# Expert rows on one core: own selection steps spread over more rows, the next selection from a later row, queries six rows apart

## What is computed

```python
def peer(h, w_query, sub_keys, u_tab, v_tab):
    def block_fn(xb):                                    # xb: tokens x 1024
        qry = (xb @ w_query).reshape(P, PEER_HEADS, 2, PEER_HALF)
        s = jnp.einsum('phcd,hckd->phck', qry, sub_keys)
        top_s, top_i = lax.top_k(s, PEER_TOPK)
        cand_s = top_s[..., 0, :, None] + top_s[..., 1, None, :]
        cand_i = top_i[..., 0, :, None] * PEER_N_KEYS + top_i[..., 1, None, :]
        best_s, pos = lax.top_k(cand_s.reshape(P, PEER_HEADS, -1), PEER_TOPK)
        idx = jnp.take_along_axis(cand_i.reshape(P, PEER_HEADS, -1), pos, axis=-1)
        gate = jax.nn.softmax(best_s, axis=-1)
        act = jax.nn.gelu(jnp.einsum('pd,phkd->phk', xb, u_tab[idx]))
        return jnp.einsum('phk,phkd->pd', gate * act, v_tab[idx])
```

## Time and profile before

| | us |
|---|---|
| median of three runs | 4306.75 (4305.49 to 4308.24) |
| the profiled execution, its own time | 4312.35 |
| its span, first to last instruction | 4310.6 |
| PE, DVE, ACT, POOL busy | 3531.4, 2658.5, 1401.6, 1209.2 |
| DMA traffic over the span | 1088.29 MB, 252 GB/s mean |
| layer 0's rows, first to last dot | 2044.8 to 3418.5 |
| layer 1's rows, first to last dot | 3623.5 to 4296.8 |

### The profile page before, as it was taken

How to read it: one execution, slowest core, us unless ns; L and a number is a source line. 1 busy time by engine, 2 the same in 40 slices (tenths; PEclk the granted TensorE clock), 3 DMA queues, 4 the chain that set the end, 5 groups by cost and what they waited for, 6 DMA issues and landing times.

```text
span 4310.6 us, 38816 instructions
## 1 busy us (share of the span) xinstructions
PE 3531.4 (82%) x11382; PEld 1864.0 (43%) x11382; DVE 2658.5 (62%) x5456; ACT 1401.6 (33%) x3747; POOL 1209.2 (28%) x1228
## 2 busy tenths in 40 slices
PE   7888978999867677778989887777888787777877
PEld 3334436844335555567545432322233255322222
DVE  3656455849656666634967577667555455786444
ACT  1231120004424544431333333433433221333333
POOL 0001100001005444520333333343435201434432
PEclk9888989999979998999999999999999998999999
DMA  5523324635321111043999999999999724999998
GB/s 214 194 78 134 120 88 171 227 149 194 130 70 33 52 52 57 23 169 150 363 379 373 371 421 421 407 418 421 410 418 416 328 79 147 387 421 421 409 421 362
DMA packets 169765, 1088.29 MB, mean 252 GB/s; under 512 B 16432, under 2 KB 45488, under 8 KB 51152
## 3 DMA queue, kind: packets, MB, share of 16 engines
q0 software_dynamic: 112608, 820.04, 46.5%
q1 hardware_dynamic: 56944, 265.77, 16.8%
HBM read 1075.19 MB, written 10.55 MB: 252 GB/s over the span
## 4 chain that ended last, share of the span: by engine, by line
PE 37%; DMA 20%; DVE 20%; issue 11%; POOL 6%; ACT 6%; DVEq 0%; SPq 0%; POOLq 0%; ACTq 0%
PE bank L199 20%; DMA arena<-in_uv,arena 17%; PE bank L2977 6%; ACT arena L211 5%; POOL arena L3009 5%; DVE arena L3026 4%; DVE arena L443 2%; PE bank L1620 2%; DVE arena L561 2%; PE bank L2454 2%; DVE arena L217 1%; PE bank L2151 1%; PE bank L2143 1%; DMA arena<-in_w_rows 1%; DMA arena<-in_wq 1%
## 5 line engine op out<-in xcount | busy, mean ns | idle before, releaser
L2977 PE MATMUL bank<-arena 128*128 128x512 f32 x3072 | 1499.6, 622 | 356.8 <-ACT arena L211 355.5
L211 ACT ACTIVATE arena<-arena 128x1 f32<-128x1 f32 (+4 forms) x2831 | 949.6, 335 | 2024.9 <-DVE arena L3026 1136.9
L199 PE MATMUL bank<-arena 128*128 128x256 f32 (+4 forms) x4640 | 1304.1, 440 | 79.8 <-ACT arena L211 33.4
L3026 DVE CUSTOM_DVE_ANT_0 arena<-arena 128x1024 f32<-128x1024 f32 x768 | 941.2, 1226 | 631.1 <-DMA arena<-in_uv,arena 602.3
L3009 POOL DMA_INDIRECT arena<-in_uv,arena x768 | 791.9, 1031 | 1289.7 <-PE bank L2977 880.5
L2977 PEld LDWEIGHTS bank<-arena 128*128 128x128 f32 x3072 | 547.9, 193 | 1281.0 <-ACT arena L211 829.3
L199 PEld LDWEIGHTS bank<-arena 128*128 128x128 f32 (+2 forms) x4640 | 808.3, 196 | 564.9 <-issue 427.4
L211 ACT ACTIVATE arena<-bank 128x512 f32<-128x512 f32 (+4 forms) x306 | 160.8, 525 | 508.9 <-PE bank L199 324.4
L443 DVE CUSTOM_DVE_ANT_0 arena<-arena 128x1024 f32<-128x1024 f32 x192 | 241.0, 1255 | 33.3 <-DMA arena<-in_w_rows 21.6
L211 ACT ACTIVATE arena<-bank,arena 128x128 f32<-128x128 f32 (+1 forms) x400 | 162.4, 406 | 290.5 <-PE bank L2143 228.1
L626 POOL TENSOR_SCALAR arena<-arena 128x1 f32<-128x1 f32 (+3 forms) x48 | 16.9, 353 | 655.6 <-ACT arena L211 459.8
(11 more groups left out here) (251 smaller groups left out, 2505.5 us busy)
## 6 DMA issues: line engine op xcount, KB each, us to landing
arena<-in_w_rows SPq DMA_DIRECT2D x50, 1024.0 KB, 5.1
arena<-in_w_in SPq DMA_DIRECT2D x16, 2048.0 KB, 7.9
arena<-in_wq SPq DMA_DIRECT2D x14, 2048.0 KB, 8.5
arena<-in_dn_w SPq DMA_DIRECT2D x12, 2048.0 KB, 10.1
arena<-in_w_up SPq DMA_DIRECT2D x11, 2048.0 KB, 8.1
arena<-in_dn_wo SPq DMA_DIRECT2D x8, 2048.0 KB, 11.0
arena<-in_w_rows POOLq DMA_DIRECT2D x14, 1024.0 KB, 5.5
arena<-decay_rest SPq DMA_DIRECT2D x56, 256.0 KB, 5.1
```

Of the source, the lines that this page charges most:

```text
L199: t = p.e.matmul(out, l, r, start=(i == 0), stop=(i == n - 1))
L211: return a().activation(out, in_, f, **kw)
L2977: t = p.e.matmul(by[half], m["dg"][ee % 4], m["uv"][r][:, 1024 + 512 * half:1536 + 512 * half], start=(ee == 0), stop=(ee == 127))
L3026: v().tensor_tensor_reduce(self.spare, uv[:, 0:1024], m["ht"][n % 2], 1.0, 0.0, ALU.mult, ALU.add, m["acts"][:, ee:ee + 1]).then_inc(*V.up ...
```

## The change

Four tables of numbers move instructions, nothing is computed otherwise.

- Own steps of tile 0 (both layers): two in every third row and one in the others (4 in 3 rows), so layer 0's end in row 54 instead of 36 and layer 1's in row 33 instead of 22.
- Tile 1's selection starts at row 60 of tile 0 instead of 40 (layer 0), with 5 steps in 3 rows instead of 5 in 4; in layer 1 at row 36 instead of 28, with 5 in 4 as before.
- Of the late steps the queries stand six rows apart from row 78 on (78 to 174) instead of four from row 76 (76 to 140). The projection and the norm stay.
- So tile 2's selection starts at row 48 of tile 1 instead of 14, with 3 steps in 2 rows instead of one a row. Every selection still hands out its indices about where it did (rows 119 and 114 against 119 and 113).

```diff
-    LATE = dict([(10 + 6 * j, j) for j in range(8)] + [(10 + 8 * 6 + 2 * j, 8 + j) for j in range(9)]
-                + [(10 + 8 * 6 + 18 + 4 * j, 17 + j) for j in range(17)])
+    LATE = dict([(10 + 6 * j, j) for j in range(8)] + [(58 + 2 * j, 8 + j) for j in range(9)]
+                + [(78 + 6 * j, 17 + j) for j in range(17)])
...
     def own_gate_row(self, layer, group):
 
-        return (self.gate_step(0, group) - self.FIRST_STEPS[layer] + 1) // 2 - 1
+        wanted = self.gate_step(0, group) - self.FIRST_STEPS[layer]
+        row = 0
+        while row + (row + 2) // 3 < wanted:
+            row += 1
+        return row - 1
+
+    def own_steps(self, ee):
+
+        return 2 if ee % 3 == 0 else 1
 
     def select_row(self, layer, n):
 
-        return {(0, 0): 40, (0, 1): max(8, max(self.LATE) - 126), (1, 0): 28}.get((layer, n), 8)
+        return {(0, 0): 60, (0, 1): max(8, max(self.LATE) - 126), (1, 0): 36}.get((layer, n), 8)
 
     def ahead_steps(self, layer, n, ee):
 
         if ee < self.select_row(layer, n):
             return 0
-        return 2 if n == 0 and ee % 4 == 0 else 1
+        once = {(0, 0): ee % 3 == 0, (0, 1): ee % 2 == 1, (1, 0): ee % 4 > 0}.get((layer, n), True)
+        return 1 if once else 2
...
                 if n == 0:
-                    for _ in range(2):
+                    for _ in range(self.own_steps(ee)):
                         next(first, None)
```

## The result

| | before | after |
|---|---|---|
| median | 4306.12 us (4304.95 to 4308.24, 4 runs) | 4277.98 us (4277.05 to 4283.94, 4 runs) |
| ratio | | 0.9931, 95% interval 0.9918 to 0.9943 |
| the profiled execution, its own time | 4312.35 | 4277.18 |
| its span | 4310.6 | 4275.4 |
| layer 0's rows, first to last dot | 1373.7 (2044.8 to 3418.5) | 1348.5 (2041.3 to 3389.8) |

The change gained 28.1 us between the medians. In the two profiled executions the rows themselves are 25.2 us shorter in layer 0 and 4.1 in layer 1, 29.3 together. The spans differ by 35.2; the 5.9 beyond the rows lie ahead of them and between the layers, where both programs are the same, so they aren't the change's.

A forecast was written before the change was run, and what follows sets the result against it. The DMA bounds the kernel, so only its idle stretches in the row stages, 37 us by busy share, can be gained. 2.2 + 5.9 + 2.8 + 2.5 - 0.5 + 4.5 = 17.4 us takes 4306.75 to 4289.4, range 4280 to 4302.

The forecast's parts named there:

- Parts 3, 4 and 5: Rows 60 to 119: denser DVE, weight wait gone, 8.3 us idle becomes 5.5 (gain 2.8); tile boundary: gain 2.5.
- Part 3's density: Layer 0, rows 60 to 119: selection in 60 rows; DVE needs 166 us, DMA 154 to 159, DVE 7 to 12 over.
- the slack: Gather buffers: DVE, ACT and PE together may be delayed 7.3 us free; only what is over it idles the DMA.
- Part 1: Tile 0's own steps, 4 in 3 rows: idle of 9.4 us becomes 7.2, gain 2.2 (0 to 4), capped by PE.
- Part 2: Tile 1's selection from row 60 instead of 40: idle of 7.4 us becomes 1.5, gain 5.9 (2.9 to 7.4).
- Part 5's cost in tile 1: Tile 1, 1.5 selection steps a row: 2.45 us a row on average, inside the slack, cost 0.5 us (0 to 2).
- Part 6: Layer 1, own steps 4 in 3 rows and select at row 36: idle 5.5 us becomes 1, gain 4.5 (1.5 to 5.5).
- DVE as the bound: Rival, rows 60 to 119: step costs or waits above the mean, idle 13 to 17 us, 4297 to 4301; chance 0.2.
- PE as the bound: Rival, rows 10 to 58: PE blocks at every late projection, gain 12, 4295; chance inside the forecast's 0.65.
- a wait for the weights that stays: Rival: load slower behind fuller gather queues (over 15 us), 2.8 and 2.5 go, 4295; chance inside the forecast's 0.65.
- Slower through query blocks: Rival, query rows up to 120: each 3.6 us query block costs its full length, 34 us idle, 4318; chance 0.05.
- All slack is used well: Rival: idle in rows 60 to 119 falls to 1 us and the select costs nothing, 4282; better case's chance 0.05.

The follow-up runs named there:

- The probes: Changed kernel with extra work of known length on DVE or on PE in layer 1's second tile; that tile takes 330.6 and 329.0 us against 315.1.
- experiment 1: Kernel before with only the queries six rows apart, and tile 2's selection from row 48 of tile 1; 4294.65 us against 4308.77, ratio 0.9967.
- experiment 7: Changed kernel with its queries four rows apart again from row 78; 4298.37 us, ratio 0.9970 to the kernel before.
- experiment 8: Changed kernel with its queries five rows apart from row 78; 4282.57 us, ratio 0.9939 to the kernel before.
- 9 and 12: Changed kernel, no query from row 121 to tile 1's row 2, then five apart, tile 2's selection at row 50; 4271.85 and 4271.34 us.
- experiment 2: Kernel before with only tile 1's selection moved to row 60, 5 steps in 3 rows; 4304.63 us, ratio 0.9991.

## Why the prediction was wrong

The sign, the places and most of the mechanisms held; the size didn't. The median lies only 2 us under the range, and 4279.95 when measured again, at its edge; but the gain was 28.1 us where 17.4 was forecast. In the rows, 29.3 less 17.4 is 11.9: the share's own reading is 22.6, so 5.2 us of this are terms that were too small in the prediction's own unit, and 6.7 are what the unit leaves out.

**The first failed step is the measure**, "So I count only what the DMA stands idle in the row stages, as width x (1 - share / 1.01)". The rows have the rate in their last column. By it the same five stretches have lost 12.2, 9.3, 14.3, 9.3 and 8.6 us, 54 instead of 37. The probes show that the share misses part of the time. The Trainium skill, "Perfetto Trace Analysis", Identifying the Most-Contended Engine, says that for DMA one should take the utilization of HBM instead of occupancy, since with 16 engines the latter misleads. The trace agrees: of 29.3 us between the dots the share shows 22.6.

**The second is what was put in place of the waits for the weights**: an idle of 5.5 us for DVE's excess in 2280 to 2400, and 4 at the boundary. By the share the changed kernel loses 2.7 in rows 80 to 120 and 2.3 in rows 0 to 20 of tile 1. And by the rate there was more to gain: the stretch with two of the three waits had lost 14.3 where the prediction has 8.3, and 2430 to 2460, behind the third, 9.3 where it has 6.5. Parts 3, 4 and 5 with tile 1's cost gave 2.8 + 2.5 - 0.5 = 4.8 us; the queries alone gave 14.2 (experiment 1), and taken out of the change they cost 16.8 (experiment 7). This is the largest term that was mis-sized, and it alone is about as large as the miss of 10.7 us between the medians.

**Part 3's density** was sized right as a sum and wrong as a price. Rows 60 to 119 took 164.9 us (2212.6 to 2377.5) where DVE's sum was 166, with 148.67 of DVE busy. But in these rows the changed kernel loses 1.4 + 5.1 + 0.9 = 7.4 us by the rate and 2.8 by the share, and experiment 1, with the old, sparser selection, loses 3.3 + 1.9 in rows 80 to 120 and next to nothing in 60 to 80: the density costs some 2 us, not the 7 to 12 less the slack. Nor did it stretch POOL's gather issues there, the second price. POOL's gathers alone in rows 60 to 119, before and after:

```profile
2230.40:2403.90 173.50, 69.68 (x58) 0.95 0.96 384
...
2212.60:2377.50 164.90, 63.29 (x60) 1.00 0.99 402
```

That is 1.20 us for an issue before and 1.05 after. What stretches an issue the traces do tell: before, the 42 issues whose first 0.93 us lay almost wholly (0.90 or more) beside a dot took 1.63 us on average, the 101 that met no DVE instruction with two tensor inputs 0.94. In rows 60 to 119 there were 13 such meetings before and 8 after, so the denser selection did not bring more of them.

Point by point for the rest:
- **Part 1**, 2.2 with bounds of 0 and 4: measured 4.6 to 6.9, by the rows 5.1, above the upper bound. Too much was taken off for PE. Rows 0 to 9, ahead of the first late projection, go from 28.3 to 23.0 us, and rows 10 to 19, where it stands, from 28.9 to 26.6; in the latter the loss by the rate falls from 8.4 to 3.2. This fits a lag of DVE that PE's block met, and not the block alone.
- **Part 2**, 5.9 (2.9 to 7.4): 4.1 alone, with the density's cost in it (interval 0 to 8); rows 40 to 60 themselves go from 10.0 to 2.3 by the rate. With Part 1 the two were to give 8.1; measured 8.8 to 10.8. POOL's waits for PE did not fall under 8 us as expected (8.70 is left), and the share rose to 1.0 all the same, since they stand apart.
- **Part 5's cost in tile 1**, 0.5 (0 to 2): 2.8 by the rate. With the last queries further ahead of the select it is 0.9 (experiment 8), 0.8 and 2.1 (9 and 12), so a good part comes from them and not from the 1.5 steps a row. The update of x was to wait 5 to 6 us; it waited 10.42, and 6.95 and 4.23 with the queries out of the way. (The 1.5 us that the prediction reads at the next boundary are 2.0 by its own formula; nothing hangs on it.)
- **Part 6**, 4.5 (1.5 to 5.5): 4.1 by the dots, 3.7 to 5.6 alone. Right within what can be measured.
- **The slack** of 7.3 us for all engines together is 5 to 6 for a block on PE, which fits 7.3 less PE's own lag; on DVE it is 2.4 to 5.5, which doesn't.
- **The rivals.** DVE as the bound, PE as the bound, and a wait for the weights that stays are all refuted by the time; the wait is 0.2 us. Slower through query blocks (4318) is refuted by it too, and by experiment 2, where the queries stand closer beside the denser selection; but the prediction's argument against it doesn't bear, since the first query starts at 2278.20 and the stretch 2200 to 2280 holds next to none. "All slack is used well" (4282) was nearest, but not for its reason: rows 60 to 119 still lose 2.8 us by the share and 7.4 by the rate, where it has 1. By its own parts the chances add up to 0.80 for faster and 0.15 for same, not 0.78 and 0.17.

## What to carry to other kernels

Where one core's DMA is the bound, take the lost time from the bytes moved against the best rate that the trace itself shows, not from the busy share; here the share missed about a microsecond of every dip. A sum of such losses over a whole stage must agree with the time, since the bytes are the same; its worth is that it says where. What a wait costs here is about what it exceeds the buffers' slack by, so spread the blocks and waits of all engines until each stands alone: halving three waits of 5 us brought the gain to 26 us, and taking them away to 30. Before moving a block ahead of another engine's pending work, look for what stands behind its first wait in that engine's order, and which bank it holds.

## What the runs showed of the hardware

- With 4 to 6 gathers of 1.05 MB in flight (tile 1 before, 2500 to 2750), the 16 DMA engines read as busy 1.01 at 421 GB/s. They also read 1.01 at 411 and 412 GB/s around blocks on other engines, 0.95 at 375, and 0.89 at 301 in the 4 us in which the gathers come again after they had run out: about the first microsecond that a block costs doesn't show in the share.
- Blocks on PE of 3.5 and 5.2 us cost nothing, of 7.0 us 1.0, of 12.2 us 7.1; from 8.7 us on each added microsecond costs 1.3 to 1.4.
- PE left idle by blocks of 4.9 us and more on DVE had a mean granted clock of 0.89 to 0.92 in these stretches, and 1.00 around the blocks of the probe that kept PE busy.
- A gather issue on POOL took 1.63 us on average when it ran beside a dot of DVE (two SBUF inputs), and 0.94 us beside none (before; 1.44 and 0.95 after).
